# Attention with the turned fp32 probabilities as stationary operand of one value product, in place of split probabilities, a split value operand and a fold

## The reference

```python
# A and B, per head; 8 blocks of 128 queries, all 1024 keys
sc = einsum('qd,sd->qs', q, k, preferred_element_type=float32) * scale
o  = einsum('qs,sd->qd', softmax(sc), v)
# C: two maps per head, with a bias that falls with distance
sc = einsum('mqd,msd->mqs', q, k) * scale - slope * dist
p  = softmax(sc)
o  = einsum('qs,sd->qd', p[0] - lam * p[1], v)
# D: per query only a neighbourhood of 8 x 16 keys, with a learned bias
o  = einsum('qn,qnd->qd', softmax(q . k_near * scale + bias), v_near)
```

## Time and profile before

| | us |
|---|---|
| median of 3 runs | 3702.86 |
| lowest and highest run | 3701.55, 3702.90 |
| span of the profiled execution, first to last instruction | 3702.0 |
| PE busy, PEld busy | 3240.0, 2703.9 |
| DVE, ACT, POOL busy | 1533.5, 1345.0, 590.2 |
| mean granted TensorE clock, share of full speed | 0.916 |

### The profile page before, as it was taken

The page is one execution under the profiler, slowest core; times in us unless marked ns, Lnnn a source line. Parts: engine busy times, 40 slices in busy tenths (PEclk is TensorE's granted clock), DMA queues, the critical chain, the costliest instruction groups (busy, mean ns, idle before and its releaser), DMA issues. The chain is left out here.

```text
span 3702.0 us, 41905 instructions
## 1 busy us (share of the span) xinstructions
PE 3240.0 (88%) x16432; PEld 2703.9 (73%) x16432; DVE 1533.5 (41%) x1889; ACT 1345.0 (36%) x2198; POOL 590.2 (16%) x275
## 2 busy tenths in 40 slices
PE   6788988887859999999769889888859699999996
PEld 5777777676748888888658778776757588888885
DVE  4848554377152111111358467443771611111115
ACT  3647644365132121212227466443640421212113
POOL 1000000111222222222210000002022222222222
PEclk9889998888879999999879999998979799999997
DMA  6030222100131111111230311221001311111112
GB/s 147 1 75 9 67 63 63 31 11 6 46 125 46 46 51 45 50 46 45 102 63 1 74 34 40 63 62 42 1 12 40 131 52 46 46 49 47 45 51 102
DMA packets 264655, 192.24 MB, mean 52 GB/s; under 512 B 64392, under 2 KB 245384, under 8 KB 264458
## 3 DMA queue, kind: packets, MB, share of 16 engines
q1 hardware_dynamic: 264510, 190.42, 19.1%
q10 hardware_dynamic: 12, 0.02, 0.0%
HBM read 142.17 MB, written 24.89 MB: 45 GB/s over the span
## 5 line engine op out<-in xcount | busy, mean ns | idle before, releaser
L240 POOL TENSOR_TENSOR w_l_m<-w_raw_m,w_h_m 128x1024 fp32r<-128x1024 f32 (+2 forms) x136 | 313.7, 2307 | 1101.1 <-ACT w_h_m L231 1100.9
L248 PE MATMUL u_ps<-h_hi,w_h_m 128*128 128x512 f32 x1024 | 406.8, 397 | 14.6 <-POOL w_l_m L240 14.6
L249 PE MATMUL u_ps<-h_lo,w_h_m 128*128 128x512 f32 x1024 | 407.2, 398 | 0.0
L249 PE MATMUL u_ps<-up_l,w_h_m 128*128 128x512 f32 x1024 | 398.4, 389 | 0.0
L248 PE MATMUL u_ps<-up_h,w_h_m 128*128 128x512 f32 x1024 | 398.4, 389 | 0.0
L231 ACT ACTIVATE w_h_m<-w_raw_m 128x1024 fp32r<-128x1024 f32 (+2 forms) x136 | 135.8, 1003 | 578.0 <-PE u_ps L252 562.6
L1614 DVE TENSOR_TENSOR mlp_out_t<-mlp_out_t,u_ps 128x1024 f32<-128x1024 f32 x64 | 78.1, 1221 | 591.8 <-PE u_ps L252 591.8
L252 PE MATMUL u_ps<-h_hi,w_l_m 128*128 128x512 f32 x1024 | 323.1, 397 | 0.0
L252 PE MATMUL u_ps<-up_h,w_l_m 128*128 128x512 f32 x1024 | 315.3, 389 | 0.0
L1604 DVE TENSOR_TENSOR m_square<-m_relu 128x1024 f32<-128x1024 f32 x64 | 78.4, 1225 | 512.8 <-ACT m_relu L1590 512.8
L248 PEld LDWEIGHTS u_ps<-h_hi,w_h_m 128*128 128x128 f32 x1024 | 193.8, 189 | 61.7 <-POOL w_l_m L240 15.4
(11 more groups left out here) (301 smaller groups left out, 6756.7 us busy)
## 6 DMA issues: line engine op xcount, KB each, us to landing
w_raw_m<-in_w_down SPq DMA_DIRECT2D x64, 512.0 KB, 4.1
w_raw_m<-in_w_up SPq DMA_DIRECT2D x56, 512.0 KB, 4.1
x_mlp_pre<-out_x SPq DMA_DIRECT2D x16, 512.0 KB, 8.9
out_x<-x_mlp_pre SPq DMA_DIRECT2D x16, 512.0 KB, 2.6
x_mlp_post<-out_x SPq DMA_DIRECT2D x16, 512.0 KB, 8.8
out_x<-x_mlp_post SPq DMA_DIRECT2D x16, 512.0 KB, 2.6
w_raw_o<-in_w_out SPq DMA_DIRECT2D x14, 512.0 KB, 4.2
x_mix_pre<-in_x SPq DMA_DIRECT2D x8, 512.0 KB, 8.2
```

The lines of the kernel that those rows point to most:

```text
L240: last = nc.gpsimd.tensor_tensor(lo[0:rows, u % 2, cols, :], raw[0:rows, u % 2, cols, :], hi[0:rows, u % 2, cols, :], ALU.subtract)
L248: nc.tensor.matmul(o, w_hi, x_hi[:, tok], start=first, stop=False)
L249: nc.tensor.matmul(o, w_hi, x_lo[:, tok], start=False, stop=False)
```

## The change

The value product is turned round. Stationary is now the turned probability block itself, `pt`, 128 keys x 128 queries in plain fp32, and moving is the value block, 128 keys x 64 in plain fp32. Eight such products (in D four or five) accumulate a tile's output, 128 queries x 64, straight into `o_ps`. There is no splitting of the probabilities: each buffer of `t_ps` is copied once, by one engine. In A, B and C the first buffer of a tile goes to ACT and the second to DVE; in D all of an even tile goes to ACT and all of an odd one to DVE. The groups of two tiles, `ot_ps`, `ot`, the lift, the fold and its matrix are gone; `o_ps` has two buffers, one a map. In the stages ahead `v_s` holds v once, and the DVE instructions that wrote its rest are gone. Both maps of a head of C are still multiplied with v separately and joined afterwards. The core of the diff:

```diff
@@ attention_stage, buffers
-                pt_h = sb(c, f"pt_h_{tag}", [P, 2, kslots, 2 * P], F32R)
-                pt_l = sb(c, f"pt_l_{tag}", [P, 2, kslots, 2 * P], F32R)
-                ot = sb(c, f"ot_{tag}", [P, 2, 2 * P])
+                pt = sb(c, f"pt_{tag}", [P, 2, kmax * P])
...
-                ot_ps = ps(c, f"ot_ps_{tag}", [P, HALF])
-                o_ps = ps(c, f"o_ps_{tag}", [P, NT, HD])
+                o_ps = ps(c, f"o_ps_{tag}", [P, 2, NT, HD])
@@ PE
                             if p >= 2:
-                                pe.wait_ge(S["pt_lo"], p - 1)
+                                pe.wait_ge(S["pt_act" if pieces[p - 2][3] == "act" else "pt_dve"], pieces[p - 2][4])
...
-                            k, cols = steps[at]
-                            for j, pt in enumerate((pt_h, pt_l)):
-                                last = nc.tensor.matmul(ot_ps[:, cols], v[:, k, :],
-                                                        pt[:, g % 2, k - base_of[i // 2], cols],
...
-                        for j in range(2):
-                            last = nc.tensor.matmul(o_ps[:, i + j, :], ot[:, g % 2, j * P:(j + 1) * P],
-                                                    fold[:, :], start=True, stop=True)
...
+                    def values(n):
...
+                        for k in range(cnt):
+                            last = nc.tensor.matmul(o_ps[:, m % 2, i, :], pt[:, n % 2, k * P:(k + 1) * P],
+                                                    maps[m][2][:, first + k, :], start=(k == 0), stop=(k == cnt - 1))
+                        last.then_inc(S["pv_done"], 1)
...
-                    for n in range(n_all + 3):
+                    for n in range(n_all + 1):
                         if n + 2 < n_all:
                             scores(n + 2)
                         if n < n_all:
                             turn(n)
-                        if 0 <= n // 2 - 1 < n_groups:
-                            values(n // 2 - 1, n % 2)
-                        if n >= 4 and n % 2 == 0:
-                            finish(n // 2 - 2)
+                        if n >= 1:
+                            values(n - 1)
@@ ACT (DVE has the same with tensor_copy and who == "dve")
+                    def lift(n):
+                        if n >= 2:
+                            act.wait_ge(S["pv_done"], n - 1)
+                        for p, (of, k0, k1, who, count) in enumerate(pieces):
+                            if of == n and who == "act":
+                                act.wait_ge(S["ptr_done"], p + 1)
+                                nc.scalar.activation(pt[:, n % 2, k0 * P:k1 * P], t_ps[:, p % 2, 0:(k1 - k0) * P],
+                                                     ACT.Copy).then_inc(S["pt_act"], 1)
@@ DVE
-                            nc.vector.tensor_tensor(pt_l[at], turned(p, k0, k1), pt_h[at], ALU.subtract) \
-                                .then_inc(S["pt_lo"], 1)
@@ pair_stage; A and B alike
-                            for n in range(2):
-                                dve.wait_ge(S["tt_hi"], n + 1)
-                                nc.vector.tensor_tensor(v_half(n, HD, P), turned(n), v_half(n, 0, HD), ALU.subtract)
@@ what copies which buffer: A, B, C, and then D
+                                        lambda n, b: "dve" if b else "act"
+                                    lambda n, b: "dve" if n % 2 else "act"
```

More of the change, by code:

```diff
@@ L465, in attention_stage, with taken @@
                 t_ps = ps(c, f"t_ps_{tag}", [P, 2, HALF])
-                ot_ps = ps(c, f"ot_ps_{tag}", [P, HALF])
-                o_ps = ps(c, f"o_ps_{tag}", [P, NT, HD])
[L469 to L479, removed]
-                    return [(piece_end[n] + b, 4 * b, min(cnt, 4 * b + 4)) for b in range(-(-cnt // 4))]
-                def turned(p, k0, k1):
-                    return t_ps[:, p % 2, 0:(k1 - k0) * P].rearrange("p (k n) -> p k n", k=k1 - k0)
+                o_ps = ps(c, f"o_ps_{tag}", [P, 2, NT, HD])
+                def taken(n, who):
+                    return sum(1 for piece in pieces if piece[0] <= n and piece[3] == who)
                 @block.tensor
@@ L611, in maximum, with lift @@
                                                            accum_out=nmax[:, n:n + 1]).then_inc(S["max_done"], 1)
-                    def split(n):
-                        m, i = seq(n)
-                        g, j = n // 2, n % 2
-                        off = tiles[i][0] - base_of[i // 2]
-                        for p, k0, k1 in pieces(n):
-                            dve.wait_ge(S["pt_hi"], p + 1)
-                            at = (slice(None), g % 2, slice(off + k0, off + k1), slice(j * P, (j + 1) * P))
-                            nc.vector.tensor_tensor(pt_l[at], turned(p, k0, k1), pt_h[at], ALU.subtract) \
-                                .then_inc(S["pt_lo"], 1)
+                    def lift(n):
+                        if n >= 2:
+                            dve.wait_ge(S["pv_done"], n - 1)
+                        for p, (of, k0, k1, who, count) in enumerate(pieces):
+                            if of == n and who == "dve":
+                                dve.wait_ge(S["ptr_done"], p + 1)
+                                nc.vector.tensor_copy(pt[:, n % 2, k0 * P:k1 * P], t_ps[:, p % 2, 0:(k1 - k0) * P]) \
+                                    .then_inc(S["pt_dve"], 1)
@@ L630, in divide @@
                                 .then_inc(S["map_done"], 1)
[L631 to L639 removed]
+                            return
@@ new lines, in divide @@
+                        nc.vector.tensor_tensor(part[:, m % 2], o_ps[:, m % 2, :, :], zb, ALU.mult) \
+                            .then_inc(S["map_done"], 1)
+                        if m % 2:
+                            dve.wait_ge(S["map_done"], m + 1)
+                            after(nc.vector.scalar_tensor_tensor(out=mix[:, :, mix_cols(m // 2)], in0=part[:, 1],
+                                                                 scalar=combine, in1=part[:, 0],
+                                                                 op0=ALU.mult, op1=ALU.add))
@@ L641, in _ @@
                     maximum(0)
                     maximum(1)
-                    for n in range(n_all + 4):
+                    for n in range(n_all + 3):
                         if n + 2 < n_all:
@@ L646, in _ @@
                         if n < n_all:
-                            split(n)
-                        if n >= NT + 3 and (n - 3) % NT == 0:
-                            divide((n - 3) // NT - 1)
+                            lift(n)
+                        if n >= NT + 2 and (n - 2) % NT == 0:
+                            divide((n - 2) // NT - 1)
             end_stage()
@@ L1085, in build @@
                              for i in range(NT)]
-                    attention_stage("d", maps, tiles, lambda m: bass.ds(pair * P + (12 * HD + m * HD), HD), mix)
+                    attention_stage("d", maps, tiles, lambda m: bass.ds(pair * P + (12 * HD + m * HD), HD), mix,
+                                    lambda n, b: "dve" if n % 2 else "act")
                 with ExitStack() as cb:
```

153 lines of the change are left out of this document (51 added, 102 removed).

## The result

The changed kernel takes 3798.41 us (median of 4 runs, 3795.77 to 3800.25) against 3702.88 (3701.55 to 3706.69) in the same session. The ratio is 1.0258, 95% interval 1.0244 to 1.0271: slower by 95.5 us. The sign was forecast and so was the mechanism of the main term; the size was not. The profiled execution spans 3798.3 us, 96.3 more than the one before.

What follows compares the result with a forecast made beforehand. PE was taken as the bound in C, and more so in A and B. Terms +165 - 12 - 8 - 4 - 11.5 + 12 gave +141 us on a span of 3702.0, forecast 3844 us, range 3810 to 3905.

Steps and rivals of the forecast that it cites:

- Value product and fold, +165: A, B, C: 1.16 us a tile removed, 16 instructions at 0.1125 added, 1.80; net +0.64 over 256 tiles, +165 us.
- rival 2: Value products: columns set the pace of short products, so 16 might take 0.93 us; time about 3610; chance 0.03.
- Rival 3: Value products: a gap between accumulating fp32 products, 0.159 an instruction, 2.54 us a tile; +353, about 4030; chance 0.05.
- All of it lies on the path, since PE has no hole to take it: A, B, C: the full +165 us of added PE time lengthens the run, over all 256 tiles.
- Ends of stages, -1 each: Ends of the 8 stages of A, B and C: without lift and fold 1 us saved each, -8 us.
- Waits of C, -12: C: PE's waits at turn, values and fold, 8.5 + 2.3 + 3.8 us, go; 12 counted.
- The copies, nothing: Copies of turned probabilities: new waits on ACT and DVE cost nothing, covered by the previous tile's 1.8 us value product.
- a failing cover: Copies: if the previous tile's value product did not cover them, a late copy would cost 0.6 to 0.7 us a tile.
- D, -4: D's 4 stages: holes take up the added products, shorter end gives -1 us each; bounds -3 and +4 a stage.
- Stages ahead, -11.5: Stretches ahead: removed subtractions for v's rest save 5.5 us in C and D, 6 in A and B, about half on path.
- The clock, +12: Stage starts: values load PE earlier at half clock, or the clock rises later; 1 us a stage, +12 us.
- Rival 1: Attention stages: clock stays at 1.2 GHz in parts; 3880 to 3960, 3944 if all four D stages; chance 0.17.

Runs made afterwards that it cites:

- two-by-two: Four kernels crossing value products of 1.79 or 0.89 us a tile with one copy a piece or ACT-then-DVE copies; changed kernel with half the products and serial copies: 3620.62 us.
- one-pass kernel: Changed kernel with turned probabilities and values kept as fp32r, low parts left out, so a value product is one instruction: 3566.48 us, 0.9632 of before.

## Why the prediction was off, step by step

- **Value product and fold, +165.** Right in kind and nearly in size. Sixteen instructions took 1.79 us for 1.80, the count was as said, and a round grew by 0.61 for 0.64; over 256 tiles 8 us less. The rejection of rival 2 held: with 32 columns a product's price doesn't change. Rival 3 (0.159 between products) didn't show.
- **"All of it lies on the path, since PE has no hole to take it".** The step that failed. It was read from a stretch in the middle of C and from a busy time that in A is 100.8 of 103.3, and applied to 32 tiles of each stage. In the first and last rounds PE did have holes: at the end of A 1.5 us in waits for the pair of copies and the lift. The first four and the last two rounds of the eight stages of A, B and C should have cost 6 x 8 x 0.61 = 29 us by their products and came out 2 us shorter than before: 31 us didn't come, where I had counted 8 for the ends. Longer products fill such holes before they cost anything. The two-by-two above shows it for the end of A: 3.58 us of longer products cost 3.14 where a piece is copied once and 1.60 where it is copied twice. For the first rounds and for C it is carried over, not shown.
- **Ends of stages, -1 each.** Mis-sized. The ends fell by 1.3 us in A and B and 2.0 in C with 1.15 us more of products in them, where my terms came to +0.3. What I had priced, the hole ahead of the last fold, was 0.76 by the run without folds. What I left out is that the turns and the last values also waited for DVE there, behind ACT, and that this chain got shorter by half.
- **Waits of C, -12.** Nearly right: the middle of C's four stages got 10 us less than its rounds give.
- **The copies, nothing.** Right in the steady rounds: PE never waits for them. The price that I gave for a failing cover was not needed, and the gain of the shorter chain at the edges, and in D, was not seen.
- **D, -4.** Direction right, size not: -9.1. Its rounds were 2.10 for 2.13 and 2.09 for the 2.09 that I worked out, so the holes did take up the products. All of the gain sits in the end, -2.6 a stage. The pair of copies put back takes all of it away, and some 2 of the 9.1 are luck with the clock (both above). Before, PE waited there (us in total, times, longest), and after the change the list is empty:

```profile
PE ot_ps_d L523 <- DVE pt_l_d L620: 0.8, 1, 0.8
PE t_ps_d L292 <- DVE pt_l_d L620: 0.8, 1, 0.8
PE o_ps_d L536 <- ACT ot_d L570: 0.5, 1, 0.5
```

- **Stages ahead, -11.5.** In C and D the eight stretches ahead fell by 0.69 us in the mean, the length of the removed subtraction, 5.5 in sum. Ahead of A nothing was gained (+0.3 in the first layer), ahead of B 0.65 in each layer: my "half of them on the path" was too much. The 2.9 us missing ahead of the second layer's A (1059.5 us from B's end; 1062.1 to 1062.4 in the kernel before and in five of the kernels above, of either kind) are no effect of the change.
- **The clock, +12.** Wrong in sign and in reason, and 12 us or more of the 45 that I was off, as much a part of the miss as the ends: without this term the forecast would have been 3832. Starting the values later again didn't bring A's or B's time back up, fewer columns cost 0.4 us at two ends of C, and when the stage started was worth up to 2.1 us. Rival 1 didn't occur: in the middle of C the granted clock is 1.00 (310 to 320, above), with turns for 0.99 of 3.12 us. The Trainium skill, page "TensorE: Matmul & The Clock Gate", section "Part 4: PE-mode transpose", says that turns don't count as activity for the clock; the 3944 and more of rival 1 didn't come. Apart from the earlier trace rows, where the clock went from the half to the full level behind sixteen turns, nothing here tests turns by themselves.

What stays open: about 3.7 us of the 7.1 by which C's rest fell have no run of their own. In C the pair of copies with half products is limited by DVE (round 2.34), so the two-by-two can't be read there. And the stretches between stages differ by up to 18 us from kernel to kernel with the same code in them.

## To carry to other kernels

Cost a change on PE by the load distance times the number of instructions, not by columns, and count an fp32 product as two: where PE sets the pace, as in A, B and C, eight narrow fp32 products (1.79 us here) lose to eight wide fp32r ones and their fold (1.16), however much they free on other engines. Then don't multiply the steady round's difference by all rounds. Read the waits at the head and the tail of the stage separately, because there PE can be the waiting engine: longer products fill holes that exist, and a shorter chain of copies pays where the products are too short to cover it, though it is free in the middle. Where a stage is short and full of holes, as D was, the same edit can win: apply it there alone.

## What was not expected of the hardware

- An instruction of a value product costs 0.111 us with 64 columns (a pass of fp32, or fp32r) and the same with 32 (fp32 alone was run); with 256 columns 0.116.
- The same stage of the same kernel starts at a mean clock of 0.53 or 0.84 over ten microseconds, according to when it starts, and differs by 1.6 to 2.1 us in length for it. Differences of one stage below that say nothing unless the clock is read beside them.
- In the kernel with half the products PE stood still six times for about 3 us in products of the MLP with nothing that the profile names; the one-pass kernel shows twelve shorter such holes, 9.5 us in sum. Both have 129 or 130 packets on the queue that the page calls "instruction", the changed kernel 108 and the kernel before 87.
